# Operand changes of a decoder block: weight sums ahead of the last staged sum, gate products behind the last low part, their gate loads behind the raw rows

## The reference

```python
h = rms_norm(z, norm_w[l])
p = (h @ w_in[l] + b_in[l]).astype(f32)
q, fz, iv, g_hg, u, g_pool, m_hg, m_pool = jnp.split(p, split_at, axis=-1)
...
y_hg = (o * jax.nn.silu(g_hg)) @ w_down_hg[l].astype(f32)
...
y_pool = (mixed * pool_scale[l].astype(f32) * jax.nn.silu(g_pool)) @ w_down_pool[l].astype(f32)
merged = jax.nn.sigmoid(m_hg) * y_hg + jax.nn.sigmoid(m_pool) * y_pool
z = z + (merged @ w_out[l].astype(f32)).astype(z.dtype)
```

## Time and profile before

| | |
|---|---|
| median of 3 runs | 1027.56 us (1025.87 to 1028.38) |
| the profiled execution | 1026.31 us |
| its span | 1024.6 us, so 1.7 us lie around it |
| PE | 1009.4 us busy, 99% |
| DVE | 810.2 us busy, 79% |
| ACT | 510.2 us busy, 50% |
| POOL | 105.7 us busy, 10% |
| DMA | 122.42 MB, mean 119 GB/s |

### The profile page before, as it was taken

How to read it: one execution, slowest core, us unless ns; L and a number is a source line. 1 busy time by engine, 2 the same in 40 slices (tenths; PEclk the granted TensorE clock), 3 DMA queues, 4 the chain that set the end, 5 groups by cost and what they waited for, 6 DMA issues and landing times.

```text
span 1024.6 us, 18569 instructions
## 1 busy us (share of the span) xinstructions
PE 1009.4 (99%) x7192; PEld 825.7 (81%) x7192; DVE 810.2 (79%) x1338; ACT 510.2 (50%) x858; POOL 105.7 (10%) x165
## 2 busy tenths in 40 slices
PE   7999999999999999999999999999999999999997
PEld 6777888888888888888888888888888878788886
DVE  7979787878787978788576778876678879988985
ACT  7764636363636353544443534343447436435665
POOL 5600000000010101010101010102110011000130
PEclk9999999999999999999999999999999999999999
DMA  8931111212020202122312131228882393568374
GB/s 322 196 103 64 43 63 43 64 39 66 22 84 22 83 22 84 24 81 73 103 42 93 48 107 43 94 82 280 298 290 95 116 337 131 178 226 335 85 155 145
DMA packets 47575, 122.42 MB, mean 119 GB/s; under 512 B 4960, under 2 KB 13152, under 8 KB 46848
## 3 DMA queue, kind: packets, MB, share of 16 engines
q1 hardware_dynamic: 24112, 72.95, 21.8%
q0 software_dynamic: 9408, 29.41, 9.7%
q10 hardware_dynamic: 13968, 18.88, 5.3%
HBM read 86.62 MB, written 29.36 MB: 113 GB/s over the span
## 4 chain that ended last, share of the span: by engine, by line
PE 86%; DVE 8%; DMA 2%; issue 2%; ACT 1%; POOL 0%; SPq 0%; DVEq 0%; ACTq 0%
PE acc L1712 71%; PE levels L1774 2%; PE miscs L1808 1%; PE miscs L1807 1%; DVE w_lo L2012 1%; PE miscs L1796 1%; PE levels L1712 1%; PE miscs L1590 1%; PE levels L1590 1%; PE acc L1656 1%; PE levels L1780 1%; DVE r_lo L2600 1%; DMA b_whole<-r_hi 1%; PE miscs L1814 1%; PE miscs L1787 1%
## 5 line engine op out<-in xcount | busy, mean ns | idle before, releaser
L1712 PE MATMUL acc<-r_hi,w_hi 128*128 128x512 f32 x1196 | 330.3, 398 | 2.8 <-ACT first L1047 0.6
L1712 PE MATMUL acc<-r_lo,w_hi 128*128 128x512 f32 x1196 | 327.7, 392 | 0.7 <-DVE r_lo L2600 0.7
L1712 PE MATMUL acc<-r_hi,w_lo 128*128 128x512 f32 x1196 | 320.6, 390 | 0.0
L1712 PEld LDWEIGHTS acc<-r_lo,w_hi 128*128 128x128 f32 x1196 | 222.1, 188 | 53.3 <-issue 4.5
L1712 PEld LDWEIGHTS acc<-r_hi,w_lo 128*128 128x128 f32 x1196 | 224.4, 188 | 48.3 <-DVE w_lo L2012 0.2
L1712 PEld LDWEIGHTS acc<-r_hi,w_hi 128*128 128x128 f32 x1196 | 217.5, 188 | 50.6 <-issue 3.1
L953 ACT ACTIVATE w_hi<-sum 128x512 fp32r<-128x512 f32 x164 | 102.0, 628 | 167.6 <-DVE sum L2045 89.7
L2012 DVE TENSOR_TENSOR w_lo<-sum,w_hi 128x512 fp32r<-128x512 f32 x164 | 111.9, 686 | 51.4 <-ACT w_hi L953 50.6
L2012 DVE TENSOR_TENSOR w_lo<-raws,w_hi 128x512 fp32r<-128x512 f32 x120 | 81.8, 686 | 47.2 <-ACT w_hi L953 47.1
L953 ACT ACTIVATE w_hi<-raws 128x512 fp32r<-128x512 f32 x120 | 74.3, 624 | 25.8 <-PE acc L1712 21.5
L1048 ACT ACTIVATE second<-acc,bias 128x512 f32<-128x512 f32 x31 | 21.3, 686 | 62.1 <-PE acc L1712 62.0
(11 more groups left out here) (328 smaller groups left out, 1309.4 us busy)
## 6 DMA issues: line engine op xcount, KB each, us to landing
raws<-in_wstream SPq DMA_DIRECT2D x80, 512.0 KB, 3.7
xin<-in_x SPq DMA_DIRECT2D x8, 512.0 KB, 5.1
a_spill<-gt POOLq DMA_DIRECT2D x16, 256.0 KB, 3.6
c_spill<-pg POOLq DMA_DIRECT2D x16, 256.0 KB, 2.7
comb<-in_wstream ACTq DMA_DIRECT2D x8, 512.0 KB, 6.7
comb_spill<-comb ACTq DMA_DIRECT2D x8, 512.0 KB, 4.9
smh_spill<-zq POOLq DMA_DIRECT2D x16, 256.0 KB, 4.4
stage<-a_spill ACTq DMA_DIRECT2D x4, 1024.0 KB, 10.4
```

What stands on the lines that cost most here:

```text
L1712: ins = pe.matmul(bank[:, :], weights, moving, start=n == 0 and i in (0, 1, y_first), stop=n == 3 * KH - 1, skip_group_check=True)
```

## The change

Three edits, in the vector engine's program and in the load queue's. The line numbers of the changed kernel are four higher behind the first edit.

```diff
@@ sync engine, loop over raw rows
                 if n == 1 and P_DH <= p:
-                    for u in range(1 if gate_first else 0, 4):
+                    if p == P_DP:
+                        load_merge(0)
+                        load_gate(14)
+                        load_gate(15)
+                    for u in range(1 if gate_first or p == P_DP else 0, 2 if p == P_DP - 1 else 4):
@@ vector engine, change(f), p = last pair before the change, q = p + 1
                 ahead(p, 3)
-                use(p, 0)
                 add_22(p)
                 operand_low(f, R_B21)
                 ahead(p, 4)
                 ahead(p, 5)
-                stage_sum(f, R_V4)
                 add_12(p)
                 weight_sums(q)
                 ahead(p, 6)
-                use(p, 1)
                 operand_low(f, R_V6)
+                stage_sum(f, R_V4)
                 ahead(q, 0)
...
                 ahead(q, 5)
+                use(p, 0)
+                use(p, 1)
                 add_12(q)
+                weight_sums(q + 1)
+                ahead(q, 6)
                 use(p, 2)
                 use(p, 3)
-                weight_sums(q + 1)
-                ahead(q, 6)
                 use(q, 0)
```

## The result

The changed kernel takes **1030.41 us** (median of 6 runs, 1029.25 to 1031.5) where the kernel before took 1026.71 beside it (6 runs, 1025.53 to 1028.38). The ratio is **1.0036, 95% interval 1.0023 to 1.0049**: 3.7 us more, a little past the 0.3% that can be told from no change. Two later comparisons of the same kernel gave 1.0026 (1.0018 to 1.0035) and 1.0030 (1.0020 to 1.0040). The forecast was 1029.5 with a range of 1026.8 to 1031.6. So the time lies in the range, the sign was right, and the size was short: +1.9 forecast, +2.5 to +3.7 measured.

What follows compares the result with a forecast made beforehand. DVE was taken to bound the second operand change, PE alone from 890 on. First change 0.0; second wins 0.6, but the late merge load makes it net +1.8, plus 0.13 restart: 1027.56 + 1.9 = 1029.5 us, range 1026.8 to 1031.6.

Steps and rivals of the forecast that it cites:

- First operand change, net 0.0: Pairs 31 and 32: moving V4's sum removes the 0.21 us wait ahead of (32,2), given back at (32,6); net 0.0.
- Second change, 0.6 won: From `add_22(35)`: without the gate product at 868.29, V4's low part and PE's (36,6) and (37,2) come 0.6 us earlier.
- The gate product ahead of `add_22(35)` was hidden: Taking it away wins nothing, since `add_22(35)` waited for PE with DVE 0.45 us idle before it.
- "No wait" for gates 14 and 15: Gate products behind (37,2)'s low part: loads have 4.3 us, landing taken as 4.0, so DVE does not wait.
- the forecast's own sign: The prediction is wrong if DVE waits for `gate_in` at the last gate products, or PE doesn't wait in pair 37.
- the rival on the late gate: Gate 15 late at DVE beyond 4.3 us of landing, delaying merge 1 and `add_22(37)`; 1030.5 to 1033.7 us; chance 0.22.
- Merge 1's release and DVE's wait: `load_merge(1)` released 3.75 us later; DVE idles some 2.6 us ahead of `merged(36,1)`; `add_22(37)` ends at 902.85.
- PE's wait ahead of (37,6): PE waits about 2.3 us for `add_22(37)`; (37,6) begins at 902.9 instead of 901.12.
- the rows of pair 38 make the loss: Experiments' rival that these later rows make the wait; the forecast had them land at 899.1 to 900, in time.
- The estimate from the page: Four merge loads and two stores land in an estimated 5.6 us instead of 7.4, giving about +0.9 instead of +1.9.
- 0.13 for the restart: Extra cost of PE's first four matmuls behind a wait, 1.20 us instead of 1.07, added for the wait at (37,6).
- The base: Median of 1027.56 us for the kernel before, 1.25 above its profiled execution, to which +1.9 was added.

Runs made afterwards that it cites:

- e1: Kernel before with only the staged sum of V4 moved, gate products and load queue as before; ratio 0.9996.
- after: The changed kernel with all its edits, in its first comparison and profiled trace, against the kernel before; 1030.41 us, ratio 1.0036.
- e2: Changed kernel with the staged sum put back, so only gate products and gate loads move; ratio 1.0027.
- e5: Changed kernel with merges 1 to 3 of pair 36 behind products 1, 3 and 5 of pair 37 instead of 0, 1 and 3; ratio 1.0005.
- e3: Changed kernel with a separate place for the second tile of merges 1 and 2, loaded ahead of gates 14 and 15; ratio 0.9996.
- e9: Changed kernel with seven extra matmuls, into a bank nothing reads, ahead of PE's wait at (37,6); ratio 1.0023.
- e4: The changed kernel again, no edit; ratio to the kernel before 1.0026.
- e10: The changed kernel a third time, no edit, run beside the kernel with the filled wait; ratio 1.0030.
- e8: Changed kernel with gate product 0 back ahead of `add_22(35)`, 1 and 2 ahead of the weight sums; merge 1 waits for 15 parts, not 16; ratio 0.9995.
- e6: From e3: gate product 0 back ahead of `add_22(35)`, product 3 behind product 2 of pair 37, pair 38's rows ahead of gate 15 and merge 3; ratio 0.9984.
- e7: Changed kernel with the load of merge 1 and all loads behind it also waiting for the first merge of pair 36; ratio 1.0029.

## Why the prediction was right in its path and short in its size

- **First operand change, net 0.0: right.** 21.83 against 21.82 us, the wait ahead of (32,2) gone and given back at (32,6). e1 shows it by itself.
- **Second change, 0.6 won: right.** V4's low part came 0.59 us earlier, in after and in e2, and not in e1. The gate product ahead of `add_22(35)` was hidden, as argued: with it gone, the idle time there grew from 0.45 to 1.03.
- **"No wait" for gates 14 and 15: wrong by half a microsecond in after, right in its repeats.** The step took a landing of 4.0 us with 4.3 at hand. In after gate 15 landed in 4.7 and DVE waited 0.47 (0.69 in e5, 0.98 in e3, 0.90 in e9); by the forecast's own sign, a wait for `gate_in` at the last gate products, that trace speaks against it. In e4, e10 and e2 the landing was 3.5 and DVE did not wait. So the step sits on an edge, at the mild end of the rival on the late gate.
- **Merge 1's release and DVE's wait: right.** The first of these issues came 4.4 us later (forecast 3.75, plus gate 15's delay), DVE waited 2.41 us (forecast 2.6) and the end of `add_22(37)` stood at 904.20, forecast 902.85 plus 1.23 of offset = 904.08. In after the landings, 3.9 and 4.5 us instead of 4.0 and 5.1, took back what gate 15 cost, so that the +1.91 there owes something to luck: two errors of opposite sign. In e4 neither error is there (gate in time, 4.0 and 5.1), and A is still 1.98 above before. PE's wait ahead of (37,6) is 1.72 to 1.94 where 2.3 was named, since PE had lost some tenths earlier in pair 37. e3 takes the wait on the part away and with it the loss; e5 and e8 take half away and keep half. That the rows of pair 38 make the loss is refuted by e3; they hold what is left there and in e5.
- **The estimate from the page.** DMA: Bandwidth & Descriptors of the Trainium skill (section Anatomy of one DMA) would have had the loads of merges 1 and 2 land soon enough for +0.9. The page gives its fit for one transfer issued from GpSimd. Here SP issued the loads, several together. From the issue of the first store beside them to the landing of the four it is 893.4 - 886.28 = 7.1 us before (the forecast's 7.4 took about 886.0), 893.87 + 4.5 - 891.32 = 7.05 in after, 7.1 in e4 and 7.7 in e10, and none is near the 5.6 of that estimate.
- **"0.13 for the restart": the step that was too small.** It was taken from waits of 0.2 to 0.4 us. In after's own trace it holds (E is 0.16 longer), but there W was 1.72. In the two repeats of the same kernel (e4, e10) W was 1.94, the granted clock fell behind it, and E was 1.63 and 1.70 longer than before: a restart of 1.6 to 1.7, not 0.13. Counted from `add_22(35)` on, the three executions pay 44.75 - 42.84 + 0.16 = 2.1 us, 44.82 - 42.84 + 1.63 = 3.6 and 45.39 - 42.84 + 1.70 = 4.3. Counted from pair 31 they pay 2.2, 2.5 and 3.4, since the scatter between the changes took 1.2 and 0.9 back in the repeats. The medians of the three comparisons lie 2.5 to 3.7 above before.
- **The base.** The forecast of 1029.5 stands on a median of 1027.56 for before. The six runs beside the changed kernel have 1026.71, 0.85 lower. So the time missed by 0.9 us only, where the difference missed by 1.8: that the time fell well inside the range is in part luck.

That the fall of the clock is in the medians is argued, not shown. Of the three traces of this kernel two have it and one does not, and e9 against e10 has the right direction with intervals that overlap. The mean granted clocks on record for the timed executions point the same way: 0.9975 over 29 executions of the changed kernel, 0.9982 over the 85 of the kernel before beside the experiments, 0.9984 over the 7 of e9. But among those 29, the 16 with a mean of 0.997 or less are hardly slower than the other 13 (medians 1030.2 and 1030.1 us), so its share of the time stays open. That the differences of the medians vary by over 1 us between the three comparisons fits the scatter ahead of the second change, which the traces show (2.4 us in where pair 31 begins).

The forecast gave 0.22 to slower by over 0.3% and 0.75 to within it. A mean of three comparisons lies at 0.31%, on the border itself.

## What to carry to other kernels

When work is moved behind a stretch whose engine is the bound, list what its results release: here a gate product whose result TensorE does not wait for released a load, and an engine that works in order stood still at that load, with the addition that PE needed behind it. Take the release away or put other work ahead of the waiting instruction (e3, e5, e6), and ask what is late next (e8). Price a new wait of PE by waits of its own length: here one of 0.4 us costs 0.13 to start again, one of 1.72 cost 0.16, and those of 1.92 to 1.94 cost over ten times that.

## What the hardware showed that I had not expected

Behind a wait of 1.92 to 1.94 us ahead of (37,6) the granted clock of TensorE fell toward its 1.2 GHz level for some eight to twelve matmuls in all four traces that have such a wait (e2, e4, e7, e10; 0.66 to 0.73 over the 5 us from 905 on), and it cost 1.6 to 1.9 us from there to the end. Behind 1.72, 1.34, 1.28 and 0.39 us (after, e5, e8, e3) it did not fall, nor in the one trace where seven matmuls filled the wait up to 0.15 (e9). Ahead of it PE had waited at most 0.65 us at a time from (36,6) on in these four traces, at a granted clock of 1.00. The Trainium skill, page TensorE: Matmul & The Clock Gate (Part 1), says that the clock is throttled when TensorE idles and released by activity; the 0.73 of e4 and the 1.00 of e9 agree with that. Whether the length of this wait decides it, or also what PE did earlier, stays open: no run varied the length alone, and 1.72 and 1.92 lie close together.
